# Recurrence loop of an RWKV-7 branch: per chunk Aa'S + MakT V is formed and multiplied by the inverse there, in place of W1T and U1 formed ahead

## The chip, the cores and the metric

The kernel runs on one core of a Trainium2 chip. The metric is the device time of the whole kernel in microseconds (us), as the median over runs. Engines: PE is the matrix engine, which loads weights (PEld) and then streams a moving operand past them; DVE is the vector engine, ACT the scalar engine, POOL and SP mostly issue DMAs here. Each engine runs its own list of instructions in order and waits on semaphores for the others.

## What is computed

Two transformer-like layers over 512 tokens of width 1024: an RWKV-7 recurrence beside dilated attention, a mixture of 32 experts, and then two further blocks. Only the recurrence is touched. For each of 8 heads (width 64) and both directions the reference does, token by token:

```
def step(S, inp):
    r_t, w_t, k_t, v_t, a_t, b_t = inp
    sa = jnp.einsum('bhij,bhj->bhi', S, a_t)
    S = S * w_t[:, :, None, :] + sa[..., None] * b_t[:, :, None, :] + v_t[..., None] * k_t[:, :, None, :]
    return S, jnp.einsum('bhij,bhj->bhi', S, r_t)
```

Within a chunk of 64 tokens the `sa` of one token depends on those of the earlier ones through a triangular matrix. Its inverse (called H below) gives all 64 at once: SA = H (Aa'S + MakT V), where S is the state at the chunk's start, Aa the scaled `a`, V the values, and MakT the masked product of keys and `a`. Then S_next = decay * (S + Kn'V + Bn'SA) and Y = R'S + Mrk'V + Mrb'SA.

## The kernel before

**Tiling.** Everything of the recurrence is held as 128x512 float32 arrays: two heads on the partitions (64 each), 512 tokens along the rows, eight chunks of 64. There are four pairs of heads (`pr` 0 to 3) and two directions (`d`); direction 1 goes through the chunks backwards. A helper `each` issues 16 matmuls of 64x64 (8 chunks, 2 heads), and `turned` does the same against an identity, which transposes every 64x64 block. One such matmul of the program is two MATMUL records in the trace, since the operands are float32.

**Stages of a pair.** *Preparation* (`rw_prep`, steps i = 5 to 28, for both directions in turn): i = 5, 6, 7 transpose Aa, Bb and Kt into An, Bn and Kn (ACT copies them out of PSUM); 8 to 12 form five masked products (DVE evicts them, with the mask); 13 is an addition; 14 to 28 are the products of the list `PRODS`: a blocked inverse (Dt2 ... R1c, QT, GT, Ha, Hb, Hc) with KV = MakT V between, and at the end U1 = H KV and W1T = An H, all copied by ACT or added by DVE. Both directions have one PSUM bank each (4 and 5), so a step waits until its direction's last product is evicted. *The loop* (`rw_loop`, s = 0 to 7) has two parts per chunk. In part 0 PE forms W1T'S (from s = 1) and adds Mrk'V and R'S to Y; DVE makes SA = W1T'S + U1 and scales the old state (`sp`). In part 1 PE forms Kn'V + Bn'SA and adds Mrb'SA to Y; DVE makes the next state S. At s = 0 the state is zero and SA is a copy of U1.

**What sets the order.** A generator, `recurrence_order`, yields the steps of all engines in one sequence; each engine runs those that concern it, in that order. Between the recurrence steps it puts pieces of independent work. `more()` is one piece of a large projection (six matmuls of 128x512, or the same at 256, of the "woven" tiles), with the tile's split into a high and a low half on ACT and DVE at every fourth piece. 136 pieces are dealt out: 19 over the preparation of a pair (17 for pair 0), two before the loop, one behind each part of the loop (16), and none in the loop of pair 3, where they are used up. `ada` is one multiply-add of a modulation vector on DVE, fed by a POOL DMA into one of two buffers (`m_in`); all 96 lie in the preparations, one per step. `norming` (9 steps), `gated` and `turned` finish the pair before. `early` prepares the next pair inside the loop: 23 steps, one behind each direction of each part. `event` takes one step of the attention's head work (a norm, a rotation `rope`, a `turn` that is four transposes on PE through the bank of Y).

**After the loop of pair 3** PE goes on with the first scores of attention, which need kT and qT. SP loads those by DMA once the last woven tile has been used, that is just ahead of that loop.

## Time and profile before

| | us |
|---|---|
| median of 3 runs | 2815.52 (2815.05 to 2817.53) |
| profiled execution, its own time | 2816.01 |
| its span, first to last instruction | 2814.2 |
| PE busy | 2700.6 (96%) |
| DVE busy | 1570.1 (56%) |
| ACT busy | 926.6 (33%) |

The profiled execution has an own time of 2816.01 us, 1.8 us more than its span. Times in rows are us from the start of the span. A row of a timeline may merge neighbours of a kind (xN); its duration runs to the end of the last one, and since matmuls are pipelined the distance between starts, not the duration, tells what one costs. "[0.46 <-DVE slot]" is idle time of the engine ahead of the row, and what ended it. The recurrence takes the span from about 110 to 613.5 us, in the order: preparation of pair 0 (woven with the projections of the recurrence itself), loop 0 (198 to 241), preparation 1 (241 to 328) and its loop, preparation 2 and its loop, preparation 3 (512 to 597), loop 3 (597 to 613.5).

### The profile page before, as it was taken

To read this page: it belongs to the slowest core of one execution; us is meant where nothing else is said; L and a number is where in the kernel's file an instruction comes from. 1 tells how busy PE (TensorE), PEld (TensorE's weight loads), DVE (VectorE), ACT (ScalarE), POOL (GpSimd) and SP (SyncE) were. 2 spreads that over 40 slices of the span, in tenths; PEclk is the share of its full clock that TensorE was granted. 3 is DMA by queue.
4 is the path that set the end of the run, shared out by engine and by line. 5 is a ranking of instruction groups with operands and counts; after the bars stand their busy time and mean duration, and the time that the engine had idled before them with its cause. 6 is when DMAs were issued, how large, how long until landed. Compare 5 with 4: busy or idle time off the path is not lost.

```text
span 2814.2 us, 46786 instructions
## 1 busy us (share of the span) xinstructions
PE 2700.6 (96%) x20072; PEld 2001.1 (71%) x20072; DVE 1570.1 (56%) x2947; ACT 926.6 (33%) x1559; POOL 137.7 (5%) x237
## 2 busy tenths in 40 slices
PE   8999999998999998999999999999999999999999
PEld 6878787876743333347777778888887777788887
DVE  5667575755444333345686566665466865634443
ACT  6233333235400100032445543223333455332231
POOL 0010100110000000000000000000000000000000
PEclk9999999999999999999999999999999999999999
DMA  5233233363599999963353336664232532233332
GB/s 165 76 111 121 88 111 110 92 231 128 208 369 426 427 426 426 426 253 112 87 113 113 122 97 195 194 195 135 80 105 79 123 117 98 79 102 97 94 99 77
DMA packets 149958, 471.74 MB, mean 168 GB/s; under 512 B 14608, under 2 KB 41856, under 8 KB 137200
## 3 DMA queue, kind: packets, MB, share of 16 engines
q1 hardware_dynamic: 114688, 367.62, 36.4%
q0 software_dynamic: 24976, 82.71, 9.4%
q10 hardware_dynamic: 10080, 18.35, 2.3%
q8 instruction: 160, 2.62, 0.4%
q14 instruction: 54, 0.44, 0.1%
HBM read 451.05 MB, written 21.51 MB: 168 GB/s over the span
## 4 chain that ended last, share of the span: by engine, by line
PE 79%; DMA 9%; DVE 7%; ACT 3%; issue 2%; SPq 0%; ACTq 0%; POOL 0%; DVEq 0%
PE psum L154 76%; DMA wslot<-in_w_gate 3%; DMA wslot<-in_w_up 3%; PE psum L157 3%; DMA m_in<-in_w_ada 1%; DVE halfL L163 1%; DMA kT<-qk_rows 1%; DVE slot L163 1%; DVE X L163 1%; ACT halfH L160 1%; DMA ring<-in_w_rwkv_out 1%; DVE vb L163 0%; DVE m_acc L169 0%; DVE gx L163 0%; DMA X<-in_x 0%
## 5 line engine op out<-in xcount | busy, mean ns | idle before, releaser
L163 DVE TENSOR_TENSOR halfL<-ring,halfH 128x1024 fp32r<-128x1024 f32 x302 | 367.9, 1220 | 538.6 <-ACT halfH L160 538.0
L160 ACT ACTIVATE halfH<-ring 128x1024 fp32r<-128x1024 f32 x302 | 317.2, 1053 | 700.9 <-PE psum L154 692.1
L154 PE MATMUL psum<-hH,halfH 128*128 128x512 f32 x1200 | 481.9, 402 | 1.9 <-DVE hL L169 1.9
L154 PE MATMUL psum<-hH,halfL 128*128 128x512 f32 x1200 | 468.8, 391 | 0.0
L154 PE MATMUL psum<-hL,halfH 128*128 128x512 f32 x1200 | 468.7, 391 | 0.0
L154 PEld LDWEIGHTS psum<-hH,halfH 128*128 128x128 f32 x1200 | 225.5, 188 | 74.6 <-issue 24.0
L154 PEld LDWEIGHTS psum<-hH,halfL 128*128 128x128 f32 x1200 | 225.7, 188 | 48.5
L154 PEld LDWEIGHTS psum<-hL,halfH 128*128 128x128 f32 x1200 | 225.9, 188 | 43.1
L154 PE MATMUL psum<-wslot,XT 128*64 128x512 f32 x1024 | 236.3, 604 | 20.5 <-DMA wslot<-in_w_gate 15.3
L154 PE MATMUL psum<-halfH,hH 128*128 128x512 f32 (+2 forms) x576 | 217.2, 377 | 2.8 <-ACT U L160 1.3
L154 PE MATMUL psum<-halfH,hL 128*128 128x512 f32 (+2 forms) x576 | 207.7, 361 | 0.0
L154 PE MATMUL psum<-halfL,hH 128*128 128x512 f32 (+2 forms) x576 | 207.7, 361 | 0.0
L154 PEld LDWEIGHTS psum<-wslot,XT 128*64 128x64 f32 x1024 | 72.8, 138 | 159.4 <-issue 145.8
L163 DVE TENSOR_TENSOR X<-X,psum 128x512 f32<-128x512 f32 x136 | 88.2, 682 | 121.2 <-PE psum L154 121.2
L154 PEld LDWEIGHTS psum<-slot,slot 64*64 64x64 f32 x4096 | 124.3, 135 | 23.9 <-issue 13.2
L154 PE MATMUL psum<-slot,slot 64*64 64x64 f32 x4096 | 132.4, 219 | 6.7 <-DVE slot L163 2.9
L154 PE MATMUL psum<-halfH,aH 128*128 128x512 f32 x352 | 136.9, 389 | 0.0
L154 PE MATMUL psum<-halfL,aH 128*128 128x512 f32 x352 | 136.9, 389 | 0.0
L154 PE MATMUL psum<-halfH,aL 128*128 128x512 f32 x352 | 136.9, 389 | 0.0
L154 PEld LDWEIGHTS psum<-halfH,hH 128*128 128x128 f32 x576 | 109.1, 189 | 29.3 <-issue 8.6
L169 DVE SCALAR_TENSOR_TENSOR m_acc<-m_in,cact,m_acc 128x512 f32<-128x512 f32 (+1 forms) x126 | 116.3, 923 | 21.6 <-DMA m_in<-in_w_ada 20.9
L154 PEld LDWEIGHTS psum<-halfH,hL 128*128 128x128 f32 x576 | 109.2, 190 | 17.0
(492 smaller groups left out, 4115.6 us busy)
## 6 DMA issues: line engine op xcount, KB each, us to landing
wslot<-in_w_gate SPq DMA_DIRECT2D x32, 2048.0 KB, 25.0
wslot<-in_w_down SPq DMA_DIRECT2D x32, 2048.0 KB, 25.9
ring<-in_w_in SPq DMA_DIRECT2D x120, 512.0 KB, 3.7
wslot<-in_w_up SPq DMA_DIRECT2D x30, 2048.0 KB, 26.5
ring<-in_w_gu SPq DMA_DIRECT2D x88, 512.0 KB, 3.7
m_in<-in_w_ada POOLq DMA_DIRECT2D x96, 256.0 KB, 3.1
m_in<-in_w_ada POOLq DMA_DIRECT2D x48, 512.0 KB, 4.8
ring<-in_w_down SPq DMA_DIRECT2D x44, 512.0 KB, 3.5
```

The lines of the kernel that those rows point to most:

```text
L154: return self.e.matmul(*a, **k)
L157: return self.e.transpose(*a, **k)
L160: return self.e.activation(*a, **k)
L163: return self.e.tensor_tensor(*a, **k)
L169: return self.e.scalar_tensor_tensor(*a, **k)
```

## The change

An, KV, U1 and W1T are no longer formed. The preparation keeps H, and has three steps fewer per pair (`N_PREP` 26, not 29) and no step 5 on PE. The loop has three parts. Part 0: MakT V + Aa'S accumulates in PSUM, then Mrk'V and R'S go to Y as before; DVE copies the sum to a new tile Wt. Part 1: Kn'V, then H Wt; DVE copies that to SA. Part 2: Bn'SA and Mrb'SA, then the next state, as in part 1 before. `more()` and `early` stand behind parts 0 and 2 only, so nothing stands between parts 1 and 2. Aa and D2 alternate between two tiles, since Aa is now read through the loop while the next pair's is written. All three results of a direction share one bank. The interleaving follows: the same 19 (17 for pair 0) woven pieces over 21 (18) preparation steps, 25 `ada` steps for the later pairs and 21 for pair 0 where each pair had 24, with the doubled `ada` at i = 6, 8, 10, 12 for pairs 1 to 3; `gated` and `turned` at 21 and 23; two events instead of one where i is a multiple of 4.

```
-    OUTS = ("R", "W1T", "U1", "Mrb", "Mrk", "Bn", "Kn")
+    OUTS = ("R", "H", "Mrb", "Mrk", "Bn", "Kn")
     G_ = [{}, {}]
-    for n, d in [("R", 0), ("W1T", 0), ("Bn", 1), ("Mrb", 0), ("Mrk", 0), ("Bn", 0), ("Kn", 0),
-                 ("R", 1), ("W1T", 1), ("U1", 1), ("Mrb", 1), ("Mrk", 1), ("U1", 0), ("Kn", 1)]:
+    for n, d in [("R", 0), ("Ab", 0), ("Bn", 1), ("Mrb", 0), ("Mrk", 0), ("Bn", 0), ("Kn", 0),
+                 ("R", 1), ("Ab", 1), ("H", 1), ("Mrb", 1), ("Mrk", 1), ("H", 0), ("Kn", 1)]:
...
+    Wt = [rk(f"Wt{d}", 64) for d in range(2)]
...
-        SL.append(dict(lw=s[0], cum=s[1], a=s[2], e3=s[3], t1=s[4], Aa=s[5], Bb=s[6], Kt=s[7], An=s[8], e1=s[9],
-                       MakT=s[0], Dm=s[1], Dt=s[2], Lt=s[3], R0=s[4], D2=s[5], Dt2=s[6], D4=s[7], R1=s[9],
-                       QT=s[2], GT=s[6], H=s[1], KV=s[5]))
+        SL.append(dict(lw=s[0], cum=s[1], a=s[2], e3=s[3], t1=s[4], Bb=s[6], Kt=s[7], MakT=s[8], e1=s[9],
+                       Dm=s[1], Dt=s[2], Lt=s[3], R0=s[4], Dt2=s[6], D4=s[7], R1=s[9], QT=s[2], GT=s[6]))
+        AB.append((s[5], G_[d]["Ab"]))
...
-             ("Ha", "GT", "R1", "R1", "GT"), ("Hb", "GT", "H", "R1", "Ha"), ("KV", "MakT", "Vn", None, "GT"),
-             ("Hc", "GT", "H", "R1", "Hb"), ("U1", "H", "KV", None, "Hc"), ("W1T", "An", "H", None, "Hc")]
-
-    BY_ACT = ("Dt2", "D2", "D4", "QT", "GT", "KV", "U1", "W1T")
+             ("Ha", "GT", "R1", "R1", "GT"), ("Hb", "GT", "H", "R1", "Ha"), ("Hc", "GT", "H", "R1", "Hb")]
+
+    BY_ACT = ("Dt2", "D2", "D4", "QT", "GT")
...
-    def piece(d, name):
+    def piece(pr, d, name):
+        if name in ("Aa", "D2"):
+            return AB[d][(pr + (name == "D2")) % 2]
...
-    TURNS = [("An", "Aa"), ("Bn", "Bb"), ("Kn", "Kt")]
+    TURNS = [("Bn", "Bb"), ("Kn", "Kt")]
...
-                 (3, 2): [("prep", 0, d, i) for i in (5, 6) for d in range(2)] + [("shift", 3)],
+                 (3, 2): [("prep", 0, d, 6) for d in range(2)] + [("shift", 3)],
...
-                if (i - 4) * 19 // 24 > (i - 5) * 19 // 24:
+                if (i - 4) * 19 // 21 > (i - 5) * 19 // 21:
...
-                if pr and i in (25, 27):
-                    yield ("gated", "turned")[(i - 25) // 2], pr - 1
-                for _ in range(2 if not pr and i in (16, 20, 24) else 1):
+                if pr and i in (21, 23):
+                    yield ("gated", "turned")[(i - 21) // 2], pr - 1
+                for _ in range(2 if i in ((16, 20, 24), (6, 8, 10, 12))[pr > 0] else 1):
                     yield "ada",
-                yield from event(i > 8)
+                for _ in range(1 + (i % 4 == 0)):
+                    yield from event(i > 8)
...
-                for part in range(2):
+                for part in range(3):
                     for d in range(2):
                         yield "loop", pr, d, s, part
-                        x = next(early, None)
+                        x = next(early, None) if part != 1 else None
                         if x:
                             yield x
-                    if pr < 3:
+                    if pr < 3 and part != 1:
...
-                if name == "KV":
-                    pe.wait_ge(*at("Vn", pr))
-                if name == "W1T":
-                    pe.wait_ge(*at("ev", pr, d, "An"))
...
-            bs, bn = CHAIN_BANKS[d]
-            Y = bank(Y_BANK)
+            Sc, b, Y, Aa = st[d][:, s % 2, :], CHAIN_BANKS[d][0], bank(Y_BANK), piece(pr, d, "Aa")
+            bw, ba, bn = (bank(b)[:, 64 * n:64 * n + 64] for n in range(3))
             if part == 0:
                 if s:
-                    clear(bs)
                     pe.wait_ge(*at("S", pr, d, s - 1))
-                    for h in HP:
-                        i = pe.matmul(bank(bs)[h, 0:64], g["W1T"][h, cc], Sc[h, :], start=True, stop=True)
-                    i.then_inc(*up(f"rw_pe{d}", "wS", pr, d, s))
-                    free[bs] = [("SA", pr, d, s)]
                 else:
-                    pe.wait_ge(*at("ev", pr, d, "W1T"))
+                    clear(b)
+                    pe.wait_ge(*at("Vn", pr))
+                    pe.wait_ge(*at("ev", pr, d, "MakT"))
                     pe.wait_ge(*at("ev", pr, d, "Kn"))
                     if d == 0:
                         clear(Y_BANK)
+                for h in HP:
+                    i = pe.matmul(bw[h, :], SL[d]["MakT"][h, cc], Vn[pr % 2][h, cc], start=True, stop=s == 0,
+                                  skip_group_check=True)
+                for h in HP[0:2 * (s > 0)]:
+                    i = pe.matmul(bw[h, :], Aa[h, cc], Sc[h, :], start=False, stop=True, skip_group_check=True)
+                i.then_inc(*up(f"rw_pe{d}", "wS", pr, d, s))
                 for h in HP:
                     pe.matmul(Y[h, cc], g["Mrk"][h, cc], Vn[pr % 2][h, cc], start=s == 0 and d == 0, stop=False,
                               skip_group_check=True)
                     if s:
                         pe.matmul(Y[h, cc], g["R"][h, cc], Sc[h, :], start=False, stop=False, skip_group_check=True)
                 return
-            if s < 7:
-                clear(bn)
+            if part == 1:
+                if not s:
+                    pe.wait_ge(*at("ev", pr, d, "Hc"))
+                pe.wait_ge(*at("W", pr, d, s))
+                for h in HP[0:2 * (s < 7)]:
+                    pe.matmul(bn[h, :], g["Kn"][h, cc], Vn[pr % 2][h, cc], start=False, stop=False, skip_group_check=True)
                 for h in HP:
-                    pe.matmul(bank(bn)[h, 0:64], g["Kn"][h, cc], Vn[pr % 2][h, cc], start=True, stop=False)
+                    i = pe.matmul(ba[h, :], g["H"][h, cc], Wt[d][h, :], start=False, stop=True, skip_group_check=True)
+                i.then_inc(*up(f"rw_pe{d}", "HW", pr, d, s))
+                return
             pe.wait_ge(*at("SA", pr, d, s))
+            free[b] = [("SA", pr, d, s)]
             if s < 7:
                 for h in HP:
-                    i = pe.matmul(bank(bn)[h, 0:64], g["Bn"][h, cc], SA[d][h, :], start=False, stop=True)
+                    i = pe.matmul(bn[h, :], g["Bn"][h, cc], SA[d][h, :], start=False, stop=True, skip_group_check=True)
                 i.then_inc(*up(f"rw_pe{d}", "dS", pr, d, s))
-                free[bn] = [("S", pr, d, s)]
...
-            bs, bn = (bank(b)[:, 0:64] for b in CHAIN_BANKS[d])
+            bw, ba, bn = (bank(CHAIN_BANKS[d][0])[:, 64 * n:64 * n + 64] for n in range(3))
             if part == 0:
-                if s:
-                    ve.wait_ge(*at("wS", pr, d, s))
-                    ve.tensor_tensor(SA[d], bs, G_[d]["U1"][:, cc], AD).then_inc(*up(D, "SA", pr, d, s))
-                    if s < 7:
-                        ve.wait_ge(*at("S", pr, d, s - 1))
-                        ve.tensor_scalar(sp_[d], Sc, end, None, M).then_inc(*up(D))
-                else:
-                    ve.wait_ge(*now(D))
-                    ve.wait_ge(*at("ev", pr, d, "U1"))
-                    if pr:
-                        ve.wait_ge(*at("Y_done", pr - 1))
-                    ve.tensor_copy(SA[d], G_[d]["U1"][:, cc]).then_inc(*up(D, "SA", pr, d, s))
+                ve.wait_ge(*at("wS", pr, d, s))
+                ve.tensor_copy(Wt[d], bw).then_inc(*up(D, "W", pr, d, s))
+                if 0 < s < 7:
+                    ve.wait_ge(*at("S", pr, d, s - 1))
+                    ve.tensor_scalar(sp_[d], Sc, end, None, M).then_inc(*up(D))
+            elif part == 1:
+                ve.wait_ge(*at("HW", pr, d, s))
+                ve.tensor_copy(SA[d], ba).then_inc(*up(D, "SA", pr, d, s))
...
```

**Where rows move, 1.** PE at the end of the preparation of pair 3, before: the rows of woven projections that stand between are left out. `Vn_94,slot` is KV (V is the moving operand, MakT the weights), `slot_145,slot_141` is U1 (KV moving, H the weights), `slot_141,slot_148` is W1T (H moving, An the weights), each once per direction; `gup` and `con,US` are `gated` and `turned` of the pair before, `colb` is the bonus step. The x16 rows are one `each` or `turned`.

```order
L154 MATMUL psum<-Vn_94,slot_140 64x64 x16
L154 MATMUL psum<-Vn_94,slot_150 64x64 x16
...
L154 MATMUL psum<-gup,US 64x64 x16
...
L154 MATMUL psum<-slot_145,slot_141 64x64 x16
L154 MATMUL psum<-slot_155,slot_151 64x64 x16
...
L154 MATMUL psum<-con,US 64x64 x16
L154 MATMUL psum<-slot_141,slot_148 64x64 x16
L154 MATMUL psum<-slot_151,slot_158 64x64 x16
...
L154 MATMUL psum<-colb,slot_144 64x1 x16
```

The same place now:

```order
L154 MATMUL psum<-gup,US 64x64 x16
L154 MATMUL psum<-slot_144,slot_145 64x64 x16
L154 MATMUL psum<-slot_154,slot_155 64x64 x16
...
L154 MATMUL psum<-con,US 64x64 x16
L154 MATMUL psum<-H_123,slot_148 64x64 x16
L154 MATMUL psum<-H_120,slot_158 64x64 x16
...
L154 MATMUL psum<-H_123,slot_148 64x64 x16
L154 MATMUL psum<-H_120,slot_158 64x64 x16
...
L154 MATMUL psum<-colb,slot_146 64x1 x16
```

The six rows of KV, U1 and W1T (`Vn_94,slot`, `slot_145,slot_141`, `slot_141,slot_148` and their twins) are gone, and the gate of the pair before (`gup`) and its transpose (`con,US`) stand three steps earlier in the inverse.

**Where rows move, 2.** PE in one chunk (s = 1) of the loop of pair 3, before; the numbers tell the directions apart (st_128, SA_132 are direction 0, st_129, SA_133 direction 1). The rows down to the first "..." are part 0 of direction 0, and from the first Kn row on it is part 1:

```order
L154 MATMUL psum<-st_128,W1T_112 64x64 x2
L154 MATMUL psum<-Vn_94,Mrk_115 64x64
L154 MATMUL psum<-st_128,R_111 64x64
...
L154 MATMUL psum<-st_129,W1T_119 64x64 x2
...
L154 MATMUL psum<-Vn_94,Kn_117 64x64 x2
L154 MATMUL psum<-SA_132,Bn_116 64x64 x2
L154 MATMUL psum<-SA_132,Mrb_114 64x64 x2
L154 MATMUL psum<-Vn_94,Kn_124 64x64 x2
L154 MATMUL psum<-SA_133,Bn_113 64x64 x2
L154 MATMUL psum<-SA_133,Mrb_121 64x64 x2
```

And now (slot_150 is MakT of direction 0, Ab_112 its Aa):

```order
L154 MATMUL psum<-Vn_94,slot_150 64x64 x2
L154 MATMUL psum<-st_128,Ab_112 64x64 x2
...
L154 MATMUL psum<-st_129,Ab_119 64x64 x2
...
L154 MATMUL psum<-Vn_94,Kn_117 64x64 x2
L154 MATMUL psum<-Wt_134,H_123 64x64 x2
L154 MATMUL psum<-Vn_94,Kn_124 64x64 x2
L154 MATMUL psum<-Wt_135,H_120 64x64 x2
L154 MATMUL psum<-SA_132,Bn_116 64x64 x2
L154 MATMUL psum<-SA_132,Mrb_114 64x64 x2
L154 MATMUL psum<-SA_133,Bn_113 64x64 x2
L154 MATMUL psum<-SA_133,Mrb_121 64x64 x2
```

Each chunk has two pairs of rows more per direction (MakT V and H Wt), and Bn'SA follows H Wt of the other direction at once.

**Where rows move, 3.** DVE in the same chunk, before:

```order
L163 TENSOR_TENSOR SA_132<-psum,U_123 128x64
L166 TENSOR_SCALAR sp_130<-st_128,ends_125 128x64
L163 TENSOR_TENSOR SA_133<-psum,U_120 128x64
L166 TENSOR_SCALAR sp_131<-st_129,ends_126 128x64
L169 SCALAR_TENSOR_TENSOR st_128<-psum,ends_125,sp_130 128x64
L169 SCALAR_TENSOR_TENSOR st_129<-psum,ends_126,sp_131 128x64
```

and now:

```order
L181 COPY Wt_134<-psum 128x64
L166 TENSOR_SCALAR sp_130<-st_128,ends_125 128x64
L181 COPY Wt_135<-psum 128x64
L166 TENSOR_SCALAR sp_131<-st_129,ends_126 128x64
L181 COPY SA_132<-psum 128x64
L181 COPY SA_133<-psum 128x64
L169 SCALAR_TENSOR_TENSOR st_128<-psum,ends_125,sp_130 128x64
L169 SCALAR_TENSOR_TENSOR st_129<-psum,ends_126,sp_131 128x64
```

The addition of U1 has become a copy, and there is one more copy per direction and chunk on the way from one state to the next.

## Rows read from the trace of the kernel before

**Rows 1.** The page: span, and PE's and DVE's busy time.
```profile
span 2814.2 us, 46786 instructions
PE 2700.6 (96%) x20072; PEld 2001.1 (71%) x20072; DVE 1570.1 (56%) x2947; ACT 926.6 (33%) x1559; POOL 137.7 (5%) x237
```

**Rows 2.** Table by stretch: from:to, length, busy time (xinstructions) per engine, clock, DMA.
```profile
197.00:241.00 44.00, 43.20 (x482) 30.32 (x480) 24.95 (x66) 14.15 (x20) 0.00 (x0) 1.00 0.26 87
597.00:614.00 17.00, 14.30 (x380) 13.30 (x376) 9.52 (x44) 1.44 (x2) 2.68 (x5) 0.90 1.00 354
...
241.00:328.00 87.00, 84.72 (x1781) 75.58 (x1780) 59.05 (x99) 28.31 (x48) 12.90 (x24) 1.00 0.42 126
```

**Rows 3.** Waits of PE, 100 to 620 us: total us, times, longest.
```profile
PE psum L154 <- DVE slot L163: 4.1, 8, 1.0
PE psum L154 <- DMA kT<-qk_rows: 2.6, 1, 2.6
```

**Rows 4.** Timeline, preparation of pair 3: start, us, engine, operation, xcount, idle before.
```profile
560.17 4.03 PE L154 MATMUL psum<-slot,slot 64*64 64x64 f32 x128
...
564.13 0.50 PE L154 MATMUL psum<-hH,halfH 128*128 128x512 f32 x1
...
565.72 2.08 PE L154 MATMUL psum<-con,slot 64*64 64x64 f32 x64
...
567.73 0.50 PE L154 MATMUL psum<-hH,halfH 128*128 128x512 f32 x1
```

**Rows 5.** Timeline, one chunk of loop 0.
```profile
223.73 0.33 PE L154 MATMUL psum<-st,W1T 64*64 64x64 f32 x4
...
224.13 0.22 DVE L163 TENSOR_TENSOR SA<-psum,U 128x64 f32<-128x64 f32 x1
...
224.63 0.50 PE L154 MATMUL psum<-hH,halfH 128*128 128x512 f32 x1
...
226.21 0.33 PE L154 MATMUL psum<-Vn,Kn 64*64 64x64 f32 x4
226.37 0.28 PE L154 MATMUL psum<-SA,Bn 64*64 64x64 f32 x4
...
226.71 0.28 DVE L169 SCALAR_TENSOR_TENSOR st<-psum,ends,sp 128x64 f32<-128x64 f32 x1 [0.71 <-PE psum L154]
```

**Rows 6.** Timeline, one chunk of loop 3.
```profile
598.65 0.33 PE L154 MATMUL psum<-st,W1T 64*64 64x64 f32 x4
...
599.00 0.24 PEld L154 LDWEIGHTS psum<-st,W1T 64*64 64x64 f32 x4
599.03 0.23 DVE L163 TENSOR_TENSOR SA<-psum,U 128x64 f32<-128x64 f32 x1
...
599.46 0.25 PEld L154 LDWEIGHTS psum<-SA,Bn 64*64 64x64 f32 x4
...
599.89 0.63 DVE L169 SCALAR_TENSOR_TENSOR st<-psum,ends,sp 128x64 f32<-128x64 f32 x2
...
600.23 0.33 PE L154 MATMUL psum<-st,W1T 64*64 64x64 f32 x4
```

**Rows 7.** Timeline, end of loop 3 and start of attention.
```profile
608.97 0.48 PE L154 MATMUL psum<-Vn,Kn 64*64 64x64 f32 x4 [2.19 <-issue]
...
612.93 0.59 PE L154 MATMUL psum<-SA,Mrb 64*64 64x64 f32 x8
...
616.17 2.08 PE L154 MATMUL psum<-kT,qT 64*128 64x256 f32 x8 [2.64 <-DMA kT<-qk_rows]
```

**Rows 8.** Loop 3 behind that gap: two neighbouring groups, and the stretch.
```profile
610.84 0.53 PE L154 MATMUL psum<-Vn,Kn 64*64 64x64 f32 x4
611.05 0.52 PE L154 MATMUL psum<-SA,Bn 64*64 64x64 f32 x4
...
610.00:612.00 2.00, 2.00 (x44) 2.00 (x44) 1.06 (x5) 0.00 (x0) 0.00 (x0) 0.51 1.03 384
```

**Rows 9.** Timeline of DVE, preparation 0: an `ada` step and a rotation.
```profile
181.69 0.75 DVE L169 SCALAR_TENSOR_TENSOR m_acc<-m_in,cact,m_acc 128x512 f32<-128x512 f32 x1 [1.63 <-DMA m_in<-in_w_ada]
...
187.70 0.28 DVE L163 TENSOR_TENSOR z_rope<-Zst,cs 128x128 f32<-128x128 f32 x1
...
189.28 0.74 DVE L169 SCALAR_TENSOR_TENSOR m_acc<-m_in,cact,m_acc 128x512 f32<-128x512 f32 x1
```

31 lines of the change are left out of this document (15 added, 16 removed).

## The prediction, made before the changed kernel ran

> **What bounds the kernel now.** I read the page first: PE is busy for 2700.6 of 2814.2 us, DVE for just over half [rows 1]. Then the table by stretch over the recurrence: PE is busy for 84.7 of 87 us in the preparation of pair 1 and for 43.2 of 44 in loop 0; only in loop 3, which has no woven projection in it, does it fall to 14.3 of 17 [rows 2]. The waits of PE over all of the recurrence name DVE's evictions with 4.1 us in eight waits, and one wait of 2.6 us for the DMA of kT [rows 3]. So the number and length of PE's small matmuls is what counts in the preparations and in loops 0 to 2. In loop 3 it is the chain state, PE, DVE, PE, DVE, next state; and behind it stands a DMA that lands later than the loop ends.
>
> **What is taken away.** One step for both directions (32 matmuls of the program, 64 records) goes from 565.72 to the next projection at 567.73, 2.01 us; two steps in a row go from 560.17 to 564.13, 3.96 us [rows 4]. A step added to a group therefore costs 3.96 - 2.01 = 1.95 us, and the changes to and from projections, some 0.1 us, stay in number, because the count of woven pieces does. Four steps (An, KV, U1, W1T) for four pairs: 16 x 1.95 = **-31.2 us**, all of it on PE, and on its path as long as PE is the bound. ACT's 32 copies go too; ACT is a third busy [rows 1] and that is worth nothing.
>
> **What is added on PE in covered loops (0 to 2).** In loop 3 the groups of two matmuls (x4) follow each other evenly: W1T of direction 0 starts at 598.65, that of direction 1, three groups later, has its weights at 599.00, so 0.117 us a group [rows 6]. Per chunk MakT V and H Wt come for two directions, four groups, 0.47 us. 3 pairs x 8 chunks x 0.47 = **+11.2 us**. The third group that is new by name, Aa'S, takes the place of W1T'S.
>
> **The new wait in covered loops.** Before, a projection of 1.6 us stands on PE behind either part (224.63 to 226.21) and covers DVE [rows 5]. Nothing stands between parts 1 and 2 now. From the start of Bn at 226.37 to DVE's next instruction at 226.71 it is 0.34 us [rows 5]; a read of 128x64 from PSUM takes 0.22 us [rows 5]; from DVE's end to PE's next group 0.06 us (the first state of the double row that starts at 599.89 is done 0.28 us later, and W1T starts at 600.23) [rows 5, 6]. Part 1 is Kn, H Wt, Kn, H Wt: H Wt of direction 0 starts at 0.16, is evicted from 0.50 to 0.72, and Bn'SA can start at 0.78; PE has issued the other three groups by 0.16 + 3 x 0.117 = 0.51. That leaves 0.27 us idle per chunk, and 0.4 in the last, which has no Kn. 3 x (7 x 0.27 + 0.4) = **+6.9 us**. Direction 1's eviction is over by the time Bn and Mrb of direction 0 are. The other copy, Wt, has a projection on PE in front of its reader and costs nothing; the cover gone, it would cost the 0.2 us of loop 3. Queued on DVE behind the copy of SA is only SA of the other direction and then the state, both for the same loop.
>
> **Loop 3.** Before, a chunk takes 600.23 - 598.65 = 1.58 us [rows 6]: 12 groups, 1.40 us, and a short wait for the state. After, with the same latencies: part 0 has eight groups, 0.94 us; H Wt of direction 0 starts at 1.05, its eviction at 1.40, Bn'SA at 1.68; the state's eviction at 2.03, and the next chunk at 2.37. So +0.79 for each of six chunks, 4.8 us. The first chunk has MakT V, a copy, H Wt and a copy where a copy of U1 stood, and must wait for the bonus product's eviction before its first matmul, since all shares one bank now: +1.3. The last one: +1.0. The loop's end moves from 613.5 to 620.6, 7.1 us later. But PE idled for 2.64 us there for kT, whose load is issued when the woven tiles are done, ahead of the loop, and so moves with the preparation and not with the loop [rows 7]. **+7.1 - 2.6 = +4.5 us.** What is late next is the loop itself: kT has landed 4 us before.
>
> **The preparations' cover.** DVE's work does not shrink: masks, norming and the 96 `ada` steps now lie over 21 steps (18 for pair 0) in place of 24 (21), and four of them are doubled where the masked products already keep DVE near PE's pace. An `ada` step is 0.75 us and may wait for its DMA first, 1.63 us in the row [rows 9]. In pair 0 both halves of a rotation and its first transpose come close: at i = 24 the transpose on PE follows, in the same step, a doubled `ada` and a rotation of 1.6 us (187.70 to 189.28) [rows 9], with one projection of 1.6 us over them, so PE waits about 2 x 0.75 + 1.6 + 0.7 (Hb's eviction) - 1.6 = 2.2 us. For pairs 1 to 3 I take 0.7 us each, from the 4.1 us in eight waits of now [rows 3], since a step that had no projection behind it at i = 9 has one now. **+4.3 us**, with bounds of 0 (the events fall into slack) and 9 (each of the 12 doubled `ada` adds its 0.75 to PE's wait).
>
> **Sum.** -31.2 + 11.2 + 6.9 + 4.5 + 4.3 = -4.3 us. From the profiled execution's own 2816.0 that is 2811.7; the median of the runs is 0.5 lower, so I forecast **2811.5 us**, 0.14% below before. A change of less than 0.2%, 5.6 us, can't be told from none in this kernel.
>
> **Rivals.** *A: the preparations absorb the denser DVE work, and the new gap closes in part.* For it: DVE is only half busy over the whole [rows 1], and PE's waits for it are small [rows 3]. Then +4.3 falls away: -8.6, and 2807; with the loop gaps at half, 2803.5. Against it: the waits that exist sit just where the doubled steps go.
> *B: slower, DVE reaches the copy of SA late.* In loops 0 to 2 the steps that prepare the next pair (512 columns wide, some 0.6 to 0.7 us each) and the splits go through DVE's queue between Wt and SA. Before, a projection hid that; now PE stands behind it. The row of 226.71 has DVE idle for 0.71 us before its eviction [rows 5], which speaks against it; if one more such instruction stood in front in each of the 24 chunks, it would cost 24 x 0.6 = 14.4 us, and the time would be 2826. It ends above before + 0.2% once the mean delay per chunk is over 0.41 us (9.9 us on top of -4.3).
> *C: the clock.* Behind the 2.19 us gap ("issue", in which PE waited for nothing that the profile shows) the granted clock of loop 3 is 0.51, the 1.2 GHz level, and a group takes 611.05 - 610.84 = 0.21 us instead of 0.117 [rows 7, 8]. If the new loop 3, with a fifth of its time idle in short waits, ran at that level throughout, a chunk would have 16 x 0.21 = 3.4 us instead of 2.37: +1.0 for seven chunks, less the some 2 us that this level costs already now, so +5, and 2816.5. The loop before kept 1.00 until that gap, with a short wait in each chunk. The Trainium skill, in "TensorE: Matmul & The Clock Gate", section "A second HAM failure mode: psum-queue depth-cycling", says that frequent micro-idles between groups of matmuls make the clock oscillate; by that rule this rival would hold, and so far the trace agrees only for the long gap.
> *D: the change does not do what it says for PE's time.* If the first steps of pairs 1 to 3 are DVE's and not PE's, taking An away there only makes PE wait: 3 x 1.95 = 5.9 us not gained, 2817.4.
>
> **How the numbers follow.** Forecast 0.40, A 0.30, B 0.15, C 0.06, D 0.09. The forecast's own range is 2808 to 2816, of which some lies below the bound of 2809.9. Faster by over 0.2% is A and a little of the forecast, 0.35; slower by over 0.2% (above 2821.2) is B and the tail of D, 0.17; within 0.2% is the rest, 0.48. The range leaves out A's lower tail and most of B: 2803 to 2823.
>
> **What the profile after would show.** PE's MATMUL records fall by 1024 and rise by 512, to about 19560. In the preparations the waits of PE for DVE: near 4 us for A, near 8 for the forecast, 12 or more for D. In loops 0 to 2 a wait of PE ahead of Bn<-SA of about 0.27 us in each chunk; over 0.6 on average is B. In loop 3 a chunk of about 2.4 us, at full clock, and no wait for kT before the first scores; 3.4 us and a clock near 0.5 is C. The forecast is wrong if a removed step turns out not to give back 1.95 us, or if the stall for instructions ("issue") in loop 3 comes twice or not at all, which is 2 us and the clock behind it either way.

## The result, and the profile after

The changed kernel takes **2827.78 us** (median of 8 runs, 2824.91 to 2833.75) against 2816.86 (2815.05 to 2823.23) before, measured beside it: ratio 1.0039, 95% interval 1.0028 to 1.005. It is slower by 10.9 us, where I had forecast 4.3 us faster and a range that ended at 2823. The profiled execution has an own time of 2827.28 us, 11.27 above that of before. Profiles also differ ahead of the changed code: the first part of the span took 109.77 us before and 107.88 after (109.89 and 109.73 in two later kernels), 1.9 us that have nothing to do with the change.

The page of after, its first lines:

```profile
span 2825.5 us, 45789 instructions
## 1 busy us (share of the span) xinstructions
PE 2696.0 (95%) x19560; PEld 1992.9 (71%) x19560; DVE 1584.2 (56%) x3011; ACT 907.8 (32%) x1527; POOL 138.3 (5%) x237
```

19560 MATMULs are what I had counted, 512 fewer than in [rows 1], yet PE is busy only 4.6 us less. So part of the work ran slowly, and the rest of the time went into waits. Both can be read stage by stage. These are tables by stretch of before and then after: from:to, length, busy time of PE and the other engines (xinstructions), granted clock, DMA share. A stage ends where the next begins; preparations and loops take turns.

```profile
109.77:194.22 84.45, 82.19 (x1491) 68.78 (x1491) 60.80 (x102) 23.09 (x37) 12.36 (x23) 1.00 0.37 111
...
327.05:375.00 47.95, 46.23 (x520) 32.83 (x519) 27.72 (x79) 14.69 (x21) 0.00 (x0) 1.00 0.24 76
375.00:462.98 87.98, 85.37 (x1714) 72.58 (x1713) 64.72 (x111) 28.16 (x45) 12.90 (x24) 1.00 0.37 116
...
511.89:596.45 84.56, 81.35 (x1697) 70.52 (x1696) 56.47 (x100) 22.13 (x37) 11.82 (x22) 1.00 0.31 96
596.45:612.93 16.48, 14.26 (x385) 13.46 (x385) 9.56 (x45) 1.88 (x2) 2.82 (x4) 0.90 0.97 343
```

```profile
107.88:190.06 82.18, 78.77 (x1302) 65.64 (x1302) 60.40 (x100) 20.32 (x32) 10.76 (x20) 0.96 0.35 107
190.06:243.08 53.02, 51.36 (x647) 37.06 (x646) 28.52 (x82) 16.11 (x22) 0.54 (x1) 1.00 0.25 81
243.08:323.46 80.38, 77.14 (x1489) 67.91 (x1489) 59.22 (x100) 22.94 (x39) 12.92 (x24) 0.98 0.44 129
323.46:381.24 57.78, 52.85 (x648) 38.15 (x647) 30.97 (x95) 14.26 (x20) 0.54 (x1) 0.97 0.21 66
381.24:466.49 85.25, 79.16 (x1456) 66.31 (x1457) 65.41 (x113) 23.96 (x38) 12.91 (x24) 0.98 0.41 125
466.49:521.71 55.22, 52.08 (x719) 42.47 (x718) 29.54 (x86) 19.94 (x32) 0.54 (x1) 1.00 0.20 64
521.71:601.78 80.07, 73.90 (x1441) 62.96 (x1441) 57.51 (x103) 17.18 (x29) 12.38 (x23) 1.00 0.36 107
601.78:626.16 24.38, 21.30 (x514) 18.98 (x513) 14.33 (x61) 1.88 (x2) 2.82 (x4) 0.93 0.91 323
```

Three terms come out of each row. The idle time is length minus PE's busy time. The clock's cost is length x (1 - clock). It holds as long as PE is the one that is waited for, and the clock is rounded to 0.01, so it is good to 0.4 us a stage. What is left is PE's work at full rate, together with the gaps between matmuls that are too short to show as idle (some 0.3 us, since the end of a pipelined matmul is modelled). Summed over the four preparations and the four loops:

| us | length | idle | clock | work |
|---|---|---|---|---|
| preparations, before | 343.09 | 10.36 | 0.0 | 332.7 |
| preparations, after | 327.88 | 18.91 | 6.6 | 302.4 |
| difference | **-15.2** | +8.5 | +6.6 | -30.4 |
| loops, before | 160.07 | 7.00 | 1.7 | 151.4 |
| loops, after | 190.40 | 12.81 | 3.4 | 174.2 |
| difference | **+30.3** | +5.8 | +1.8 | +22.7 |

-15.2 + 30.3 is +15.1; less 1.9 for the start and 2.7 for the wait for kT, which is gone (kT's first matmul follows loop 3 at 626.73 with no wait, where [rows 7] had 2.64), that is +10.6 at kT's first matmul, and 0.7 more come behind it. **The work moved nearly as forecast; the clock (+8.4) and longer waits of PE for DVE did most of the rest.** For the loops the forecast had +25.2 (11.2 + 6.9 + 7.1), and without the clock they grew by 28.5.

The clock can be checked on all runs, not only on the two profiles: the mean clock over the whole kernel was 0.9893 in the 8 runs of the changed kernel and 0.9910 in the 83 runs of the kernel before that were taken beside the experiments, a difference worth 5 us. That agrees with 8.4 less the stretch of low clock behind the old wait for kT (0.70 over the 10 us from 616.17, about 3 us), which the changed kernel hasn't got (1.00 over the 10 us from 626.73). That stretch cost nothing that shows: what follows kT's first matmul took 2198.0 us before and 2198.8 after.

Where the waits are: the longest ones of after (timeline of PE: start, us, engine, operation, xcount, idle before and what ended it), and the largest totals in the view of waits (total us, times, longest).

```profile
183.02 1.09 PE L157 MATMUL psum<-con,Zst 128*128 128x128 f32 x4 [3.41 <-DVE Zst L163]
...
263.21 0.76 PE L157 MATMUL psum<-con,Zst 128*128 128x128 f32 x4 [1.86 <-DVE slot L163]
...
351.23 0.33 PE L154 MATMUL psum<-SA,Bn 64*64 64x64 f32 x4 [2.31 <-DVE SA L181]
...
426.57 0.62 PE L154 MATMUL psum<-Ab,slot 64*64 64x64 f32 x14 [2.30 <-DVE slot L163]
```
```profile
PE psum L154 <- DVE slot L163: 5.5, 5, 2.3
PE psum L157 <- DVE Zst L163: 4.8, 2, 3.4
PE psum L154 <- DVE SA L181: 4.5, 7, 2.3
```

Before, the longest wait for DVE in the recurrence was 1.1 us (at 486.38 and 533.40). Around each of these four the granted clock drops to 0.50 or near it (0.55 at the third), the 1.2 GHz level. Around the first, by stretch, and the product that ran there (its 64 records take 3.68 us; in [rows 4] as many of the same size take 2.08):

```profile
182.00:184.00 2.00, 0.98 (x4) 0.72 (x4) 0.81 (x3) 0.00 (x0) 0.12 (x1) 0.50 0.78 246
184.00:186.00 2.00, 2.00 (x37) 1.97 (x38) 0.00 (x0) 1.38 (x2) 0.00 (x0) 0.50 0.21 73
186.00:188.00 2.00, 2.00 (x35) 1.88 (x32) 0.93 (x2) 0.36 (x1) 0.00 (x0) 0.50 0.21 77
...
264.00:266.00 2.00, 2.00 (x40) 2.00 (x42) 1.41 (x4) 1.38 (x3) 0.37 (x1) 0.50 0.13 49
```
```profile
184.04 3.68 PE L154 MATMUL psum<-H,slot 64*64 64x64 f32 x64
```

And the steady part of a loop. First a chunk of loop 0 (PE), which answers to [rows 5], then one of loop 3, which answers to [rows 6]:

```profile
219.69 0.33 PE L154 MATMUL psum<-Vn,Kn 64*64 64x64 f32 x4
...
220.09 0.28 PE L154 MATMUL psum<-Wt,H 64*64 64x64 f32 x4
220.47 0.33 PE L154 MATMUL psum<-SA,Bn 64*64 64x64 f32 x4
...
225.38 0.33 PE L154 MATMUL psum<-Vn,Kn 64*64 64x64 f32 x4
```
```profile
618.31 0.33 PE L154 MATMUL psum<-Vn,slot 64*64 64x64 f32 x4
...
620.77 0.33 PE L154 MATMUL psum<-Vn,slot 64*64 64x64 f32 x4
```

The chunk in loop 0 takes 225.38 - 219.69 = 5.69 us, 0.77 more than before's 4.92 (forecast 0.74). The gap between parts 1 and 2 is 220.47 - 220.09 less a group of 0.117, 0.26 us (forecast 0.27). In loop 3 it is 2.46 us (forecast 2.37).

### The profile page after: what moved, and what is told of

Its sections match the earlier page's. It is cut to its first block, busy times and chain, and to the rows that moved or that the text cites. A ratio compares the mean times of both kernels' runs of the same rounds, so it can differ in the third digit from the quotient of the medians.

```text
span 2825.5 us, 45789 instructions
## 1 busy us (share of the span) xinstructions
PE 2696.0 (95%) x19560; PEld 1992.9 (71%) x19560; DVE 1584.2 (56%) x3011; ACT 907.8 (32%) x1527; POOL 138.3 (5%) x237
## 4 chain that ended last, share of the span: by engine, by line
PE 78%; DMA 9%; DVE 8%; ACT 3%; issue 2%; SPq 0%; POOL 0%; ACTq 0%; DVEq 0%
PE psum L154 75%; DMA wslot<-in_w_gate 3%; DMA wslot<-in_w_up 3%; PE psum L157 3%; DMA m_in<-in_w_ada 1%; DVE halfL L163 1%; ACT halfH L160 1%; DVE m_acc L169 1%; DVE X L163 1%; DMA ring<-in_w_rwkv_out 1%; DVE slot L163 1%; DVE vb L163 0%; DVE n_ht L169 0%; DVE gx L163 0%; DVE US L163 0%
## 5 line engine op out<-in xcount | busy, mean ns | idle before, releaser
L169 DVE SCALAR_TENSOR_TENSOR m_acc<-m_in,cact,m_acc 128x512 f32<-128x512 f32 (+1 forms) x126 | 116.3, 923 | 23.0 <-DMA m_in<-in_w_ada 21.7
L154 PEld LDWEIGHTS psum<-halfL,hH 128*128 128x128 f32 x576 | 109.2, 190 | 14.2
L154 PE MATMUL psum<-wslot,aT 128*64 128x512 f32 x512 | 113.4, 595 | 4.1 <-ACT aT L160 4.1
## 6 DMA issues: line engine op xcount, KB each, us to landing
wslot<-in_w_gate SPq DMA_DIRECT2D x32, 2048.0 KB, 25.2
```

Source lines behind the costliest of these rows:

```text
L154: return self.e.matmul(*a, **k)
L169: return self.e.scalar_tensor_tensor(*a, **k)
```

## Experiments

All variants start from the changed kernel. Stage lengths in the text are measured as above, from one profiled execution each.

### e1_slots24: the same operations in the interleaving of before

```
-    N_PREP = 14 + len(PRODS)
+    N_PREP = 29
...
-                if (i - 4) * 19 // 21 > (i - 5) * 19 // 21:
+                if (i - 4) * 19 // 24 > (i - 5) * 19 // 24:
...
-                for _ in range(2 if i in ((16, 20, 24), (6, 8, 10, 12))[pr > 0] else 1):
+                for _ in range(2 if not pr and i in (16, 20, 24) else 1):
                     yield "ada",
-                for _ in range(1 + (i % 4 == 0)):
-                    yield from event(i > 8)
+                yield from event(i > 8)
```

> The changed kernel's operations in the interleaving of the kernel before: 24 preparation steps again (the steps of An, KV, U1 and W1T stand empty), one ada step each, gated and turned at 25 and 27, one event a step. Nothing is computed otherwise. Theory 1 (the preparations lost their gain to the denser order: DVE late, long PE waits, and a lower clock behind them): each preparation is shorter than before by 7 to 7.8 us, 10 us less than the changed kernel in all, 2817 us. Rival (a removed step of 64 records does not give back 1.95 us): the preparations stay as in the changed kernel, 2827.

2820.0 us (10 runs), 1.0008 of before, interval 0.9998 to 1.0018. The last three preparations are 9.1, 10.0 and 9.5 us shorter than before's, so a removed step gives back its 1.95 us and more. All four together are 30.3 us shorter, against 15.2 in the changed kernel. But the loops grew by 37.2 instead of 30.3. Of these 6.9 us more, 4.7 are clock (8.2 us in place of 3.4) and 2.8 idle time. Part of DVE's lag had moved past the end of the preparation, and the longest waits were these:

```profile
189.52 0.88 PE L157 MATMUL psum<-con,Zst 128*128 128x128 f32 x3 [4.09 <-DVE Zst L163]
...
354.00 0.33 PE L154 MATMUL psum<-SA,Bn 64*64 64x64 f32 x4 [2.32 <-DVE SA L181]
...
595.39 0.36 PE L154 MATMUL psum<-Vn,slot 64*64 64x64 f32 x4 [2.60 <-DVE bon L181]
```

The denser interleaving thus costs about 8 us of the 11, the theory's side; its 2817 was 3 us too low. The rest lies in single places of DVE's queue.

One thing more is to be read here. In the preparation of pair 2 DVE is busy for 62.5 of 78.0 us, 80%, more than in the changed kernel (65.4 of 85.3, 77%), and yet PE is idle for 1.2 us there and not 6.1. So it isn't DVE's share of the stage that makes PE wait, but how its instructions are spread over the steps: one `ada` behind each step here, 25 over 21 steps there.

### e4_shift1: one woven piece less at the end of loop 1

```
-                for _ in range(2):
+                for _ in range(3 if pr == 1 else 2):
                     yield from more()
...
-                    if pr < 3 and part != 1:
+                    if pr < 3 and part != 1 and (pr, s, part) != (1, 7, 2):
```

> The changed kernel with three woven pieces ahead of loop 1 and 15 in it instead of two and 16, so that the tile's split on DVE and ACT falls behind the third part of a chunk and not between Wt and the copy of SA. Theory 2 (loop 1 is 3.8 us longer than loops 0 and 2 by the split that stands in DVE's queue ahead of SA, waiting for ACT): loop 1's waits of 0.9, 2.3 and 0.3 us and the clock behind them go, -3.5 to -5 us. Rival (the rotations in loop 1 are what delays DVE): -1 at most.

2828.87 us, 1.0043 (1.0029 to 1.0057): nothing gained, as the rival had it. The split of a weight tile (`halfL`, 1.2 us on DVE) no longer stands ahead of the copy of SA. It stands, with the rotation behind it, ahead of Wt, and PE waits for that:

```profile
349.12 0.33 PE L154 MATMUL psum<-Vn,Kn 64*64 64x64 f32 x4 [2.09 <-DVE Wt L181]
```

My reading, that it was the split's place before SA which cost, fell. DVE is late there as a whole. What makes it late, e6_moved shows.

### e5_stagger: direction 1 one part behind direction 0

The idea was to cover the gap between parts 1 and 2 with the other direction's part.

```
+            for t in range(25):
+                s, part = t // 3, t % 3
+                if t < 24:
+                    yield "loop", pr, 0, s, part
...
+                if t:
+                    yield "loop", pr, 1, (t - 1) // 3, (t - 1) % 3
...
+                if pr < 3 and part != 1 and t < 24:
+                    yield from more()
```

> The changed kernel with direction 1 one part behind direction 0 in the loops, woven pieces still two per chunk. Between H Wt of one direction and Bn'SA of it now stands part 0 of the other. Theory 3 (PE waits 0.27 us per chunk between parts 1 and 2 for want of cover, and loop 3 is a chain of three round trips): loops 0 to 2 shorter by 2.3 us each, loop 3 from 2.4 to about 2.1 us a chunk, -9 us in all. Rival (the chunk's length is PE work, or DVE's queue, and not the gap): -2 us or less.

2836.63 us, 1.0071 (1.0053 to 1.0089): slower, by 9 us against the changed kernel. The quiet chunks are indeed shorter, 5.44 to 5.53 us instead of 5.69, but the two directions now ask DVE at different times, each time with an early step of 0.7 us or a split ahead in its queue, and loops 1 and 2 took 64.3 and 59.7 us (57.8 and 55.2 before this edit, without a last woven piece of 1.6 us that the new order puts inside the loop). Of this the clock has the larger part: 0.89 over loop 1 and 0.94 over loop 2, 7.1 and 3.6 us, where the changed kernel has 1.7 and 0. One of the long waits:

```profile
354.28 0.48 PE L154 MATMUL psum<-SA,Bn 64*64 64x64 f32 x4 [3.00 <-DVE SA L181]
```

### e3_ada_late: the doubled ada steps behind the masked products

```
-                for _ in range(2 if i in ((16, 20, 24), (6, 8, 10, 12))[pr > 0] else 1):
+                for _ in range(2 if i in ((16, 20, 24), (15, 17, 19, 21))[pr > 0] else 1):
```

> The changed kernel with the doubled ada steps of pairs 1 to 3 at steps 15, 17, 19 and 21 of the preparation instead of 6, 8, 10 and 12. Nothing is added or left out. Theory: the PE waits of the masked products (263.21 1.86 us, 414.87 1.33, 426.57 2.30, 540.41 1.59, 545.47 1.39; together 8.5, in the kernel before 4.6 at the like places) come from the two ada steps that stand between DVE's masks there, where DVE also has the norming of the pair before. They go back to the 0.8 to 1.1 of before, and the stretches at the 1.2 GHz level behind two of them go too: preparations 1 to 3 shorten by 1 to 2.5 us each, and the time is 2821 to 2824. Rival: the ada steps are bound by their DMAs (DVE waited 5.5 to 7 us for m_in in each of these preparations), and the same waits turn up at steps 15 to 21, where the products with identity added are as short of slack: 2826 to 2831.

2826.98 us, 1.0031 (1.002 to 1.0043): the rival. The waits at the masked products went back to 0.8 to 1.1 us, and came again later, longer:

```profile
424.17 1.12 PE L154 MATMUL psum<-Ab,slot 64*64 64x64 f32 x16 [3.60 <-DVE slot L163]
...
563.72 0.59 PE L154 MATMUL psum<-slot,slot 64*64 64x64 f32 x9 [2.17 <-DVE slot L163]
```

Loop 1 was not touched by this edit, nor by that of e10_thin below: the three kernels run the same instructions there, with the same waits (0.93 and 2.31 or 2.32 us for SA) and the same idle time (4.93, 4.94 and 4.92 us). Changed kernel 57.78 us at a clock of 0.97; e3_ada_late, then e10_thin:

```profile
322.90:379.19 56.29, 51.35 (x647) 37.06 (x646) 30.93 (x95) 14.26 (x20) 0.54 (x1) 1.00 0.21 67
```
```profile
319.04:378.41 59.37, 54.45 (x648) 39.02 (x647) 30.31 (x93) 14.26 (x20) 0.17 (x1) 0.94 0.20 62
```

So the same wait of 2.3 us was followed by a low clock in the changed kernel and not in e3_ada_late, and between profiles the clock alone moves this loop by 3 us. A clock's cost of one stage in one profile is to be read with that in mind.

### e6_moved: two events out of the two worst places

```
-                    yield from event(i > 8)
+                    yield from event(i > 8 and (pr > 0 or i < 24))
...
-                yield from event(False)
+                if (pr, s) != (1, 1):
+                    yield from event(False)
```

> The changed kernel with two events of the woven head work taken from where PE waited longest. In the preparation of pair 0 the turns of Zst no longer follow the rotation by one step; they stand in the preparation of pair 1. In loop 1 the second rotation moves one chunk later, away from the two scans and exps of the early steps. Nothing is added or left out. Theory 'queue': the waits of 3.41 us (183.02, Zst) and 2.31 us (351.23, SA) come from the place of these instructions in DVE's order alone; both go and nothing takes their place, preparation 0 shortens from 82.15 us (107.88 to 190.06) by 3.4 and loop 1 from 57.78 by 2.3. The same theory with the clock: PE runs at the 1.2 GHz level for some us behind each of the two waits (the 64 matmuls of one product took 3.68 us instead of 2.08), so a further 1.6 to 3 and about 1 come back; preparation 0 shortens by 5 to 6.4, loop 1 by 3.3, and the time falls from 2827.8 by 8 to 10, to 2818 to 2820. Rival 'chain': DVE has as much work as before and the next step that needs it waits as long; the stages shorten by under 1 us each and the time stays at 2826 to 2829.

2821.62 us, 1.001 (1.0001 to 1.002), 6 us better than the changed kernel, between the theory's 2818 to 2820 and the rival's 2826. Preparation 0 is the cleanest reading of this study:

```profile
109.89:185.74 75.85, 75.34 (x1295) 62.54 (x1295) 58.07 (x98) 20.90 (x32) 10.75 (x20) 1.00 0.37 111
```

75.85 us instead of 82.18. Idle falls from 3.41 to 0.51, the clock's 3.29 (0.96 of 82.18 us) to 0, and the work stays at 75.3. **Half of what the wait had cost was the clock.** (Of the four other profiles with this wait, 3.23 to 3.41 us, two have the same 0.96 in this stage, e4_shift1 and e5_stagger 0.98: there it cost half as much.) Loop 1 gained only 1.1, all of it idle time, and preparation 1, into which the turns had moved, lost 2.1:

```profile
349.41 0.33 PE L154 MATMUL psum<-SA,Bn 64*64 64x64 f32 x4 [1.14 <-DVE SA L181]
```

In the changed kernel DVE and ACT stand so there (timelines of both):

```profile
348.74 1.04 ACT L160 ACTIVATE halfH<-ring 128x1024 fp32r<-128x1024 f32 x1
...
349.81 1.23 DVE L163 TENSOR_TENSOR halfL<-ring,halfH 128x1024 fp32r<-128x1024 f32 x1 [0.89 <-ACT halfH L160]
350.95 0.34 DVE L181 COPY SA<-psum 128x64 f32<-128x64 f32 x2
```

The rotation (six small instructions, 1.3 us) made the early step late on which an activation of ACT waited (1.39 us at 348.20, and 0.22 without the rotation). Behind this activation ACT had the high half, behind that DVE the split, and behind that PE its SA. Without the rotation about half of the wait is left.

### e7_noH: the loop without the multiply by H

```
-                pe.wait_ge(*at("W", pr, d, s))
...
-                for h in HP:
-                    i = pe.matmul(ba[h, :], g["H"][h, cc], Wt[d][h, :], start=False, stop=True, skip_group_check=True)
-                i.then_inc(*up(f"rw_pe{d}", "HW", pr, d, s))
...
-                ve.tensor_copy(Wt[d], bw).then_inc(*up(D, "W", pr, d, s))
+                ve.tensor_copy(SA[d], bw).then_inc(*up(D, "SA", pr, d, s))
```

(Kn V stands in part 2, behind the wait for SA.)

> The changed kernel without the multiply by the inverse in the loop: SA is the copy of Aa'S + MakT V out of PSUM, part 1 of a chunk is empty, Kn V stands behind the wait for SA. The product with H (16 matmuls x 8 chunks x 4 pairs, in two directions) and the copy of Wt are left out, so the output is not the reference's. It prices what the change adds to the loops. By the prediction's terms, part 1 of a covered chunk costs 0.74 us (0.47 of PE and 0.27 of a gap) and of loop 3 0.89: the loops shorten from 53.02, 57.78, 55.22 and 24.38 to about 47, 49.5, 49 and 17.3, close to before's 46.73, 47.95, 48.91 and 16.48, and the time is 2827.8 - 27 + 2.6 (the wait for kT is back) = 2801 to 2806. If the loops' excess over the prediction (3.8 in loop 1) is from DVE's longer order and not from the third part, loop 1 keeps it: about 52. Rival: the shared bank for both directions' three slices costs by itself (waits for a free bank); then the loops stay 1 to 2 us over before's each even without the multiply.

2808.89 us, 0.9971 (0.9959 to 0.9983). The loops took 48.45, 49.36, 50.30 and 20.55 us; I had expected 47, 49.5, 49 and 17.3, and a time of 2801 to 2806. In loops 0, 2 and 3 this was 1.9 us too low each by a slip of the expectation: it took away all four new groups of a chunk, 0.47 us, though MakT V stays. In loop 3 the stalls put down to "issue" are 1.66 and 2.15 us, where the changed kernel has 1.35 and 1.08; and the wait for kT did not come back (kT starts at 606.21, right behind the loop). In the terms of the account (length, then PE's busy time; the clock is next to last but one):

```profile
190.01:238.46 48.45, 47.77 (x583) 34.57 (x582) 25.24 (x66) 16.11 (x22) 0.54 (x1) 1.00 0.27 86
...
585.10:605.65 20.55, 16.36 (x450) 15.49 (x451) 10.78 (x45) 1.88 (x2) 2.82 (x4) 0.92 0.95 337
```

The four loops' work is 159.1 us: 7.7 above before's 151.4, which is MakT V (2 groups x 0.117 x 32 chunks = 7.5). It is 15.0 below the changed kernel's, which is H Wt (again 7.5) and 7.5 us of gap, 0.23 a chunk; a part of the gap more stands under idle. By length, loop 0 fell by 4.57 us, 0.57 a chunk, which leaves 0.34 beyond the two groups of H Wt, somewhat more than the gap of 0.27. So the terms of the forecast for PE in loops 0 to 2 were right in kind and nearly in size. Loops 0 and 2 are no longer than before's plus MakT V (48.6 and 50.8), so the shared bank costs nothing that these rows would show. Loop 1 has no wait over 0.6 us here: its 2.3 us appear only where a third part makes PE ask for SA sooner behind DVE's queue.

### e10_thin: DVE's ada steps cut to 8 columns

```
-                    ve.scalar_tensor_tensor(out=acc, in0=m_in[n % 2], scalar=cact[:, k:k + 1], in1=acc, op0=M,
-                                            op1=AD).then_inc(*up(D, "m_used", L, n))
+                    c = 512 * L + 512 if L else 8
+                    ve.scalar_tensor_tensor(out=acc[:, 0:c], in0=m_in[n % 2][:, 0:c], scalar=cact[:, k:k + 1],
+                                            in1=acc[:, 0:c], op0=M, op1=AD).then_inc(*up(D, "m_used", L, n))
```

> The changed kernel with 84 of the 96 first-layer ada steps cut on DVE from 512 columns to 8 (0.75 us to about 0.1 each); the first of each eight, the transposes, the sums and all DMAs stay. Most of the product with w_ada is left out, so the output is not the reference's. It tells DVE's time from the waits for m_in. Theory 'DVE's time': the PE waits of the preparations (3.41 in pair 0, 3.2, 6.1 and 6.2 us in pairs 1 to 3) come from DVE having 22 to 25 ada steps of 0.75 us in 80 us; they fall to under 1 us each and the stretches at the 1.2 GHz level in preparations 0 to 2 go: 2827.8 - 15 = 2811 to 2815. Rival 'm_in': DVE stands in its queue until m_in has landed (12.5 us of waits for it in 243 to 462, and 5.1 in e1_slots24), and the DMAs are as late as before since their two buffers come free only after the step before the last: DVE waits longer for m_in by what it computes less, and the time stays within 4 us of 2827.8.

2817.77 us, 1.0002 (0.999 to 1.0014): 10 us less than the changed kernel, where the theory had 13 to 17 and the rival under 4. The two rows are the group of these steps on DVE between 240 and 625 us, changed kernel and e10_thin (busy us, mean ns | idle before, of which for the DMA):

```profile
L169 DVE SCALAR_TENSOR_TENSOR m_acc<-m_in,cact,m_acc 128x512 f32<-128x512 f32 x66 | 49.3, 746 | 19.5 <-DMA m_in<-in_w_ada 18.5
```
```profile
L169 DVE SCALAR_TENSOR_TENSOR m_acc<-m_in,cact,m_acc 128x8 f32<-128x8 f32 x66 | 14.6, 222 | 30.3 <-DMA m_in<-in_w_ada 29.7
```

DVE's time fell by 34.7 us there, its waits for `m_in` grew by 11.2. PE's idle time in the preparations fell from 18.9 to 12.3 us and the clock's cost from 6.6 to 1.6. So most of the lag comes from DVE's own time in these steps. It is not all: DVE in its queue waits longer for `m_in` by a third of what it saves, and with a third less of DVE's work PE still had single waits of 2.43 us (181.83) and 1.61 (422.42). Over the whole kernel the waits for `m_in` hardly differ between before and after (20.9 and 21.7 us), so they are not what the change added.

### e8_best, e9_mixed: the waits of e1 removed, then pair 0 left dense

e8_best is e1_slots24 with three moves:

```
-                for _ in range(2 if not pr and i in (16, 20, 24) else 1):
+                for _ in range(2 if i in ((16, 20, 24), (), (), (18,))[pr] else (pr, i) != (3, 28)):
...
-                yield from event(i > 8)
+                yield from event(i > 8 and (pr > 0 or i < 26))
...
-                yield from event(False)
+                if (pr, s) != (1, 1):
+                    yield from event(False)
```

> The kernel of e1_slots24 (the changed operations in the 24-step interleaving of before; 2820.0 us, 1.0008 of before) with three moves: the turns of pair 0 leave the step behind the rotation (its wait was 4.09 us at 189.52), the second rotation of loop 1 stands one chunk later (2.32 us at 354.00), and the last ada step of pair 3, which stood with its m_in wait, transpose and sum ahead of the copy of bon (2.60 us at 595.39), is doubled into step 18. Nothing is left out. If these waits are from the order alone, 9.0 us of waits and 2 to 4 us of PE at the 1.2 GHz level behind them go, less what DVE is late with at the next step: 2808 to 2812, ratio 0.996 to 0.998, faster than before. Rival 'chain': DVE's lag reaches the first chunk of the loops anyway; the waits turn up at bon and at the first Wt: 2817 to 2820, ratio 1.000 to 1.001.

2818.87 us, 1.0001 (0.9992 to 1.001): the rival. Each of the three waits went or halved, but that of pair 0 came back one step later, at the bonus, and with it a mean clock of 0.91 in loop 0, which took 59.98 us:

```profile
192.32 0.48 PE L154 MATMUL psum<-Vn,slot 64*64 64x64 f32 x4 [3.21 <-DVE bon L181]
```

e9_mixed prepares pair 0 in 21 steps, as e6_moved, and the other pairs in 24:

```
-            for i in range(i0, N_PREP):
+            for i in range(i0, N_PREP if pr else 26):
...
+                for _ in range(2 if i in ((16, 20, 24), (14,), (14,), (14, 18))[pr] else (pr, i) != (3, 28)):
```

> Pair 0 prepared as in e6_moved (21 steps, the turns of Zst moved out of it: 75.85 us without a wait over 0.6 but the first, and no stretch at the 1.2 GHz level), pairs 1 to 3 as in e8_best (24 steps: preparations of 76.8, 79.6 and 76.0), with one ada step more at step 14 of each of them, so that there are 96 again. Nothing is left out. Theory: DVE's lag is a matter of each preparation by itself, so the stage times add: from pair 0's first wait (109.9) 75.9 + 53.1 + 76.8 + 57.5 + 79 + 56 + 76 + 25.6 puts kT at 609 to 612 (before 616.17, after 626.73, e8_best 617.65), and the time at 2809 to 2813, ratio 0.997 to 0.9985. Rival: the three ada steps more in pairs 1 to 3 cost their waits for m_in and the lag shows at bon or in the loops: 2815 to 2818, ratio 0.999 to 1.000.

2813.93 us, **0.9985** (0.9976 to 0.9994), the first complete version that is faster than the kernel before, at the slow end of what the theory had. kT started at 613.98, 2 us later than the best case that I had written down: stages do not quite add. Loop 0 took its 53.08 us of e6_moved, but preparations 1 to 3 took 79.9, 80.2 and 78.1 us instead of 76.8, 79.6 and 76.0, with an ada step more in each. With that one doubled step in each, PE's idle time in these three is 11.8 us in place of 6.3.

### e11_cover, e12_cover1: which of the gaps the woven pieces cover

```
-                        x = next(early, None) if part != 1 else None
+                        x = next(early, None) if part != 2 else None
...
-                    if pr < 3 and part != 1:
+                    if pr < 3 and part != 2:
```

> The kernel of e9_mixed with the woven pieces and the early steps of a chunk of loops 0 to 2 behind parts 0 and 1 instead of parts 0 and 2: the copy of SA is covered by a piece, the new state is not. Nothing is left out. Theory (the prediction's term of the gap): between parts 1 and 2 PE waits 0.27 us a chunk for the copy of SA, whereas between part 2 and the next part 0 loop 3 shows almost none (before, 1.58 us a chunk with 12 groups of 0.117, which leaves 0.17 for both gaps). The covered loops shorten by 0.15 to 0.25 a chunk, 24 chunks, 4 to 6 us, and the time is that of e9_mixed less as much. Rival: DVE has the new state, its scaled copy and an early step in its queue at the end of a chunk, so PE waits there 0.3 us or more: no change within 2 us, or 2 to 4 us slower.

2814.57 us, 0.999 (0.998 to 1.0): no gain over e9_mixed. Loop 1 went from 58.19 to 54.48, loops 0 and 2 from 53.08 and 55.23 to 57.51 and 59.95. (With this order the last woven piece, 1.6 us, falls inside the loop as I measure it, and no longer into the preparation behind it: like for like loop 1 gained 5.3 and the others lost 2.8 and 3.1, which is no gain in all, as the time says.) Where the state is not covered, its eviction is late behind a split that waits for ACT (one wait of 3.22 us in loop 2). e12_cover1 is e9_mixed with this order in loop 1 alone:

> The kernel of e9_mixed (2813.9 us, ratio 0.9985) with the woven pieces and early steps behind parts 0 and 1 in loop 1 alone; loops 0 and 2 keep them behind parts 0 and 2. Nothing is left out. In e11_cover, which had the order changed in all three, loop 1 took 54.48 us instead of 58.19, but loop 0 57.51 instead of 53.08 and loop 2 59.95 instead of 55.23. Theory: the loops are independent in this, loop 1 keeps its 3.7 us (of which 3.5 are the stretch at the 1.2 GHz level behind the SA wait of its first chunk), kT starts at 610.3 instead of 613.98, and the time is 2809 to 2812, ratio 0.9970 to 0.9980. Rival: kT's matmuls then wait for their DMA again, as in the kernel before, where they started at 616.17 after a wait of 2.64 us for it; then at most 1 to 2 us are left of it: 2812 to 2814, ratio 0.998 to 0.999.

2811.10 us (11 runs) against 2817.43: **0.998** (0.997 to 0.9991), the lowest ratio of this study, as the theory had it. Its interval overlaps with that of e9_mixed, so that it is faster than e9_mixed is likely but not shown by the times. Its loop 1 beside that of e9_mixed:

```profile
320.74:375.22 54.48, 52.84 (x654) 38.10 (x653) 31.45 (x97) 14.68 (x21) 1.08 (x2) 1.00 0.24 78
```
```profile
316.91:375.10 58.19, 54.44 (x648) 38.94 (x647) 31.95 (x97) 14.68 (x21) 1.08 (x2) 0.94 0.23 73
```

The difference is 3.7 us, or 5.3 with the woven piece, and most is again the clock: 0.06 x 58.19 = 3.5 us. Both profiles with this order, e11_cover and this one, have 1.00 there, and neither has the wait of 0.93 us for the first SA; but since loop 1 has come out at 1.00 with the old order too (e3_ada_late), two profiles don't show that the order keeps the clock up. The 2.1 us less of idle time come from the order itself. No wait for kT returned; it started at 611.59, right behind the loop.

## Why the prediction was wrong, point by point

- **The work taken away, -31.2: right.** The account has -30.4 in the preparations, and e1_slots24 shows the stages 9 to 10 us shorter for pairs 1 to 3, once DVE's work lies as loosely as before.
- **PE's work and the gap in the loops, +11.2 and +6.9: right, if a little low.** Loops 0 and 2 grew by 6.29 and 6.31, forecast 6.04; the gap between parts 1 and 2 is 0.26 us for 0.27 in the chunk shown, and e7_noH finds 7.7 us for MakT V, where 7.5 follow from 0.117 us a group.
- **Loop 3, +7.1 - 2.6: right in kind, 0.7 low.** It grew by 7.9, and kT's wait is gone. "issue" came twice (1.35 and 1.08 us) where it had been 2.19 once.
- **The preparations' cover, +4.3 with bounds 0 and 9: the step that failed.** As idle time it was +8.5, at the upper bound, and with the clock behind it +15.1. I had charged 0.7 us a pair for pairs 1 to 3; the idle time grew by 1.0, 3.5 and 3.0 us (by 1.15 in pair 0, where I had 2.2). The base of the 0.7 was misread: 4.1 us in eight waits [rows 3] is one group of the view, and all waits of PE for DVE there come to 12.8 us before and 24.1 after. And they were the waits of an order with one `ada` a step. Three experiments show what the denser order did. The order of before, with one `ada` a step, takes the idle time of these three stages from 15.5 to 4.5 us (e1_slots24). A smaller `ada` takes it to 9.8 (e10_thin). Moving the doubled ones takes the waits along (e3_ada_late: 15.2). So it isn't the masked products' place, with which I had argued, but that more of DVE's work stands between two steps that PE waits for.
- **What the sum lacked: the clock, +8.4.** I had it as a rival for loop 3 alone (C). It came in the preparations (+6.6) and in loop 1 (+1.7), behind waits of 1.86 to 3.41 us. The forecast had the upper end of its waits in the range, but no clock behind them. With 6.6 us of it behind the upper bound of 9, the term would have been 15.6 and the time 2823, the end of the range. How much of it comes is in part chance: half of the waits of this length had none behind them (last section).
- **Rival A, the preparations absorb the denser work: false.** DVE's busy share of the whole kernel, the argument for it, says nothing about single steps.
- **Rival B, DVE late at the copy of SA: true in one loop.** Loop 1 grew by 9.83, of which 3.8 are beyond the forecast: 2.1 of waits and 1.7 of clock. It was not the 0.6 us in each chunk that the rival had priced, but waits of 2.31 us at 351.23 and 0.93 at 333.97. That its 2826 lies close to the measured time is luck. My reason against B was a row of loop 0; in loop 1 events are in the queue too.
- **Rival C: false for loop 3.** Its clock was low for about 4 us (604 to 608), as long as before [rows 8]. For the rest, though a chunk of 2.46 us holds 16 groups of 0.117 and so 0.6 us of short gaps, the stretch reads as

```profile
610.00:612.00 2.00, 1.92 (x52) 1.58 (x52) 1.32 (x6) 0.00 (x0) 0.00 (x0) 1.00 1.04 405
...
618.00:620.00 2.00, 2.00 (x58) 1.80 (x56) 1.65 (x8) 0.00 (x0) 0.00 (x0) 1.00 1.04 382
```

  at 2.4 GHz. By the Trainium skill ("TensorE: Matmul & The Clock Gate", section "A second HAM failure mode: psum-queue depth-cycling") frequent micro-idles between groups made the clock of another kernel oscillate. Short gaps of this size did not do so in these stretches, nor anywhere in loop 3 of e3_ada_late, which had 1.00 over its 24.48 us. The section puts the loss on the re-throttling and re-warming between bursts, and behind the four waits shown above the time was lost in that way, after the gap rather than in it.
- **Rival D, the first steps are DVE's, so that An's removal gives nothing: false.** Its sign came, over 18 us of waits for DVE in the preparations where I had set 12 or more, but not its mechanism: in the first 16 us of the preparations of pairs 1 to 3 of the changed kernel PE is busy for 15.99, 16.00 and 15.57 us (16.00 each before), and in e1_slots24 these stages give back 9.1 to 10.0 us, where D leaves 5.9.
- **A slip of the sum:** 2816.0 - 4.3 - 0.5 is 2811.2, and not 2811.5.

## What to carry over

When work is taken from the engine that bounds a kernel, the engine next to it keeps its work and has fewer steps to do it in. Don't judge that by its busy share, of the span or even of the stage: count what it has to do between two steps that the bounding engine waits for, and spread its instructions again, at best one a step. Read all groups of a view of waits before taking one as the base of a price. A long wait may be paid for twice here, the second time in the clock behind it: in all ten cases from 3 us on, and in half of those from 1.8 to 2.6. And look at what stands in the in-order queue of the engine that serves a new dependence, in each loop and not in a typical one, since here two chunks of one loop held most of the excess.

## What the runs showed of the hardware

- The granted clock fell to the 1.2 GHz level within the wait of 3.41 us and stayed there for 4 us of full work behind it (182 to 188: 0.50). In the 12 profiles with the change there are ten waits of PE for DVE of 3.00 to 4.09 us in the recurrence, and behind all ten the clock was low within 4 us.
- Of the 26 such waits of 1.81 to 2.61 us, 13 had a low clock within 4 us behind them and 13 did not. The length does not tell them apart: 1.86 us had it in one profile (263.21, changed kernel) and not in another (258.58, e7_noH), and so had 2.31 us. What does is open.
- A long wait is not needed. The wait of 0.93 us for the first SA of loop 1 stands in eight profiles, and in six of them the clock fell within 5 us behind it; in the changed kernel (333.97) and e3_ada_late it did not. In e9_mixed it stands at 327.38:

```profile
328.00:332.00 4.00, 3.60 (x13) 1.21 (x13) 1.41 (x8) 1.05 (x2) 0.00 (x0) 0.73 0.45 131
```

- It is not the same in every run. Loop 0 has the same instructions in e9_mixed and e12_cover1. It took 53.08 us at clock 1.00 in the one, with a wait of 0.70 us ahead of it, and 54.67 at 0.97 in the other, with 1.09. Of the 29 runs of the kernel before that were taken beside e10_thin, the fastest took 2810.60 us at a mean clock of 0.994, the slowest 2824.39 at 0.988.
- What drops the clock in loop 3, where most versions show a few us at 0.50 and e3_ada_late none, was not tried.
